# An encoder layer in float32: the residual comes back in eight halves, and VectorE's order is changed where passes meet

## What is computed

```
h = rmsnorm(x, mix_norm_g)
x = x + forgetting_attention(h, ...)          # called x1 below
h = rmsnorm(x, ffn_norm_g)
gate, up = split(h @ w_gu)                    # 2048 -> 2 * 5632
x = x + (silu(gate) * up) @ w_down            # 5632 -> 2048
```

## Time and profile before

| what | value |
|---|---|
| median of 3 runs | 2190.46 us (2188.57 to 2190.71) |
| the profiled execution's own time | 2189.52 us |
| its span in the profile | 2187.8 us |
| TensorE busy | 2129.5 us, 97% of the span |
| TensorE weight loads busy | 1852.7 us, 85% |
| VectorE busy | 1524.6 us, 70% |
| ScalarE busy | 915.4 us, 42% |
| GpSimd busy | 183.8 us, 8% |
| granted TensorE clock, mean | 0.992 |

### The profile page before, as it was taken

One profiled execution on the slowest core, in us unless ns is written; L12 is line 12 of the kernel. 1 busy time (PEld: TensorE's weight loads), 2 busy tenths in 40 slices (PEclk: granted clock), 3 DMA queues, 4 the chain that ended last, 5 costly groups with the idle time before them and its releaser, 6 DMA issues.

```text
span 2187.8 us, 27845 instructions
## 1 busy us (share of the span) xinstructions
PE 2129.5 (97%) x10404; PEld 1852.7 (85%) x10404; DVE 1524.6 (70%) x2103; ACT 915.4 (42%) x1225; POOL 183.8 (8%) x356
## 2 busy tenths in 40 slices
PE   9999999999999999999999999999999989999997
PEld 8999999999998887888888888888887777777786
DVE  4544444444464445987888888788798888898888
ACT  5433333333343334444444444444445534444432
POOL 0322213222230000000000000000000001000000
PEclk9999999999999999999999999999999999999999
DMA  6332333333343335566566566567668757757755
GB/s 181 88 92 82 88 85 90 85 89 81 92 144 135 116 106 163 178 226 220 179 222 226 177 219 229 190 207 228 193 207 280 261 201 270 236 177 250 234 175 178
DMA packets 258331, 376.30 MB, mean 172 GB/s; under 512 B 15762, under 2 KB 114100, under 8 KB 257220
## 3 DMA queue, kind: packets, MB, share of 16 engines
q1 hardware_dynamic: 254864, 354.90, 51.6%
q10 hardware_dynamic: 3380, 20.21, 2.2%
HBM read 346.45 MB, written 28.61 MB: 171 GB/s over the span
## 4 chain that ended last, share of the span: by engine, by line
PE 83%; DVE 9%; DMA 6%; issue 1%; SPq 1%; POOL 0%; ACT 0%; DVEq 0%; POOLq 0%; ACTq 0%
PE gemm L522 11%; PE gemm L524 11%; PE gemm L523 11%; PE gemm L723 8%; PE gemm L725 8%; PE gemm L724 8%; PE aux L723 7%; PE aux L725 7%; PE aux L724 6%; DVE f_lo L1344 4%; DMA f_raw<-in_ffn_w_gate_up 3%; DMA f_raw<-in_ffn_w_down 2%; DVE f_raw L1350 2%; PE aux L523 1%; PE aux L524 1%; PE aux L522 1%
## 5 line engine op out<-in xcount | busy, mean ns | idle before, releaser
L1344 DVE TENSOR_TENSOR f_lo<-f_raw,f_hi 128x2048 fp32r<-128x2048 f32 (+1 forms) x264 | 534.2, 2030 | 63.9 <-ACT f_hi L1007 51.4
L522 PE MATMUL gemm<-w_hi,act_t 128*128 128x384 f32 (+2 forms) x1280 | 450.6, 352 | 1.6 <-DVE w_lo L1123 1.6
L524 PE MATMUL gemm<-w_hi,act_t 128*128 128x384 f32 (+2 forms) x1280 | 444.0, 347 | 0.0
L523 PE MATMUL gemm<-w_lo,act_t 128*128 128x384 f32 (+2 forms) x1280 | 443.9, 347 | 0.0
L723 PE MATMUL gemm<-f_hi,a_form 128*128 128x512 f32 x1056 | 412.4, 391 | 0.4 <-DVE rows L1428 0.4
L724 PE MATMUL gemm<-f_lo,a_form 128*128 128x512 f32 x1056 | 411.7, 390 | 0.0
L725 PE MATMUL gemm<-f_hi,a_form 128*128 128x512 f32 x1056 | 411.3, 389 | 0.0
L723 PE MATMUL aux<-f_hi,a_form 128*128 128x512 f32 x792 | 318.3, 402 | 42.8 <-DVE f_lo L1344 42.8
L725 PE MATMUL aux<-f_hi,a_form 128*128 128x512 f32 x792 | 312.2, 394 | 0.0
L724 PE MATMUL aux<-f_lo,a_form 128*128 128x512 f32 x792 | 311.9, 394 | 0.0
L1123 DVE TENSOR_TENSOR w_lo<-w_raw,w_hi 128x768 fp32r<-128x768 f32 (+1 forms) x160 | 160.8, 1009 | 208.5 <-ACT w_hi L818 208.5
(11 more groups left out here) (161 smaller groups left out, 2143.0 us busy)
## 6 DMA issues: line engine op xcount, KB each, us to landing
f_raw<-in_ffn_w_gate_up SPq DMA_DIRECT2D x264, 512.0 KB, 4.2
f_raw<-in_ffn_w_down SPq DMA_DIRECT2D x132, 512.0 KB, 4.8
w_raw<-in_fox_w_in SPq DMA_DIRECT2D x192, 256.0 KB, 3.4
f_raw<-in_ffn_w_gate_up SPq DMA_DIRECT2D x88, 256.0 KB, 4.0
w_raw<-in_fox_w_out SPq DMA_DIRECT2D x16, 1024.0 KB, 5.1
a_raw<-forms_scratch SPq DMA_DIRECT2D x22, 512.0 KB, 6.3
f_raw<-in_ffn_w_down SPq DMA_DIRECT2D x44, 256.0 KB, 4.8
forms_scratch<-fa_a ACTq DMA_DIRECT2D x11, 896.0 KB, 6.3
```

Of the source, the lines that this page charges most:

```text
L522: mm(out, a_hi, b_hi, start=first, stop=False)
L523: mm(out, a_hi, b_lo, start=False, stop=False)
L524: return mm(out, a_lo, b_hi, start=False, stop=last)
L1344: v.tensor_tensor(f_lo[:, n % 4, 0:3 + g], f_raw[:, n % 4, 0:3 + g], f32(f_hi[:, n % 3, 0:3 + g]), ALU.subtract).then_inc(f_lo_done, 1)
```

## The change

It has three parts. The staging buffers in `rows` are laid out anew, with a new one, `fa_first`, for the seventh step of round 0. The residual comes back in eight loads of 512 KB, each half a column group, put behind the weight loads of eight different units, from unit 168 (round 10) to unit 195 (round 12). In VectorE's order the turn of the first pass's last unit becomes a meeting turn, and `add_p1` is cut in two: its first addition is made in turn 2 of the second pass, the other (`turn_x4`) stays in turn 4.

```
-        fa_a = at("fa_a", AREA_S, [P, 8, HW])
-        c_one = at("c_one", AREA_S, [P, 2, CW])
-        u_two = at("u_two", AREA_S + 4096, [P, 2, CW])
-        fa_b = at("fa_b", AREA_S + 8192, [P, 8, HW])
-        c_neg = at("c_neg", AREA_S + 24576, [P, 2, CW])
+        c_neg = at("c_neg", AREA_S, [P, 2, CW])
+        fa_first = at("fa_first", AREA_S, [P, 8, HW])
+        fa_a = at("fa_a", AREA_S + 8192, [P, 8, HW])
+        c_one = at("c_one", AREA_S + 8192, [P, 2, CW])
+        u_two = at("u_two", AREA_S + 12288, [P, 2, CW])
+        fa_b = at("fa_b", AREA_S + 24576, [P, 8, HW])
...
+            def reload_x1(d, half):
+                ts = slice(2 * half, 2 * half + 2)
+                sp.dma_start(rows[:, d, ts], dram_x1[d][:, ts]).then_inc(x1_ld[d], 16)
...
-                if n == BASE[R_DOWN] + 8:
+                if n == BASE[R_DOWN] - 8:
                     for d in range(ND):
                         sp.wait_ge(x1_stored[d], 16)
+                    reload_x1(0, 1)
+                if n == BASE[R_DOWN] + 6:
+                    sp.wait_ge(hidden_done, 4 * NP)
+                    reload_x1(0, 0)
+                if n == BASE[R_DOWN] + 8:
                     sp.wait_ge(hidden_tr, 4 * NP)
-                    sp.dma_start(rows[:, 2], dram_x1[2]).then_inc(x1_ld[2], 16)
+                    reload_x1(2, 1)
                 if n == BASE[R_DOWN] + 9:
+                    reload_x1(2, 0)
+                if n == BASE[R_DOWN] + 13:
                     sp.wait_ge(forms_stored[0], 16 * NP)
-                    sp.dma_start(rows[:, 0], dram_x1[0]).then_inc(x1_ld[0], 16)
-                if n == BASE[R_DOWN] + 18:
+                    reload_x1(1, 0)
+                if n == BASE[R_DOWN] + 15:
+                    reload_x1(1, 1)
+                if n == BASE[R_DOWN] + 17:
                     sp.wait_ge(forms_stored[1], 16 * NP)
-                    sp.dma_start(rows[:, 1], dram_x1[1]).then_inc(x1_ld[1], 16)
-                    sp.dma_start(rows[:, 3], dram_x1[3]).then_inc(x1_ld[3], 16)
+                    reload_x1(3, 1)
+                if n == BASE[R_DOWN] + 19:
+                    reload_x1(3, 0)
...
-                pool.wait_ge(x1_ld[n], 16)
-                pool.wait_ge(x1_ld[2 + n], 16)
+                pool.wait_ge(x1_ld[n], 32)
+                pool.wait_ge(x1_ld[2 + n], 32)
...
-                x1, x4 = rows[:, n, 0:2], rows[:, 2 + n, 2:4]
+                x1 = rows[:, n, 0:2]
                 v.tensor_tensor(x1, x1, junk_act[:], ALU.add).then_inc(x1_p12, 1)
+
+            def turn_x4(r):
+                n = (r - R_DOWN) % 2
+                x4 = rows[:, 2 + n, 2:4]
                 v.tensor_tensor(x4, junk_act[:], x4, ALU.subtract).then_inc(x4_p1, 1)
...
-                meeting = (g == 0 and j == ROUND_K[r] - 2) or (g == 1 and j == 0)
+
+                form = LOAD_AT.get(n - 4)
+                if g == 0 and j == ROUND_K[r] - 2:
+                    form = None
+                if g == 0 and last and n - 5 in LOAD_AT:
+                    down_forms_lo(*LOAD_AT[n - 5])
+                meeting = (g == 0 and j >= ROUND_K[r] - 2) or (g == 1 and j == 0)
...
+                    if r >= R_DOWN and j == 2:
+                        add_p1(r)
                     if r >= R_DOWN and j == 4:
-                        add_p1(r)
+                        turn_x4(r)
...
-                if n - 4 in LOAD_AT:
-                    down_forms_lo(*LOAD_AT[n - 4])
+                if form:
+                    down_forms_lo(*form)
```

More of the change, by code:

```diff
@@ L950, in form_read @@
                 if q >= 6:
-                    act.wait_ge(x1_stored[q - 6], 16)
+                    act.wait_ge(x1_stored[7 - q], 16)
                 k = NK + 4 * d + i
@@ L1018, in read_p1 @@
                 if r == 0:
-                    act.wait_ge(x1_stored[0], 16)
+                    act.wait_ge(x1_stored[1], 16)
                     act.wait_ge(aform_lo, 7)
@@ L1053, in hidden_forms @@
                     act.wait_ge(forms_stored[1], 16 * (r - 1))
+                if i == 1 and r == 1:
+                    act.wait_ge(x1_stored[3], 16)
                 for half, pair in ((0, slice(0, 8, 7)), (1, slice(1, 7, 5))):
@@ L1091, in _ @@
                         form_hi(6, fa_a)
-                        form_read(7, fa_b)
+                        form_read(7, fa_first)
                     if r == 0 and j == 3:
-                        form_hi(7, fa_b)
+                        form_hi(7, fa_first)
                     if j == 3 and hidden:
@@ L1367, in second_pass_read @@
                     dve.wait_ge(x1_stored[2], 16)
-                    dve.wait_ge(x1_stored[3], 16)
                 for t in range(2):
@@ L1419, in add_p2_p3 @@
                 if r < R_DOWN + 2:
-                    dve.wait_ge(x1_ld[n], 16)
+                    dve.wait_ge(x1_ld[n], 32)
                 for t in range(2):
@@ L1520, in _ @@
                             form_lo(6, fa_a)
-                            form_sums(7, fa_b)
+                            form_sums(7, fa_first)
                         if j == 3:
-                            form_lo(7, fa_b)
+                            form_lo(7, fa_first)
                             row_sums(1)
```

## The result

| | before | after |
|---|---|---|
| median | 2190.59 us (2188.57 to 2191.37, 4 runs) | 2205.93 us (2201.93 to 2207.18, 4 runs) |
| profiled execution, its span | 2189.52, 2187.8 us | 2205.96, 2204.2 us |
| granted TensorE clock, mean | 0.992 | 0.994 |

The ratio is 1.0068, 95% interval 1.0051 to 1.0086: the change makes the kernel slower, by more than the 0.2% that can be told from nothing. Four executions among those of the experiments, two of them of the kernel before, took 3442 to 5674 us; medians and ratios here leave them out.

What follows compares the result with a forecast made beforehand. TensorE was taken as the bound, busy 2129.5 of 2187.8 us, losing time only through waits, clock or added work. The terms 19.6 - 4.5 - 5.5 = +9.6 us on the 2190.46 us median gave 2200 us, range 2193 to 2209.

Steps and rivals of the forecast that it cites:

- The swap: Where the two passes meet, rounds 0 to 10: `f_lo` goes ahead of the next unit's sums; +19.6 us, ends +15 and +24.
- 2.5 - 1.08: Round 1's meeting: 2.5 us of delay less 1.08 us gained by `f_lo` of the second pass's first unit starting sooner.
- P1's wait: Middle of the second pass's first unit: TensorE waits 1.3 us for ScalarE's late copy of P1.
- The echoes: After P1's wait: TensorE's waits for `f_lo` of the next two units, 0.55 and 0.45 us.
- Round 11, -4.5 us: Round 11: earlier `f_lo` and load, and part of the slow clock won back; -4.5 us, ends -2 and -7.
- GpSimd's two additions take 2.38 each: Round 11's meeting: after the last half's estimated landing at 1752.5, both additions end at 1757.3.
- on an engine with room inside the pass: 0: VectorE: the first addition of `add_p1` moves two turns ahead, the same 1.22 us each, costing 0.
- Rounds 12 to 16, -5.5 us: Rounds 12 to 16: meeting waits replaced by shorter ones, -2, and slow clock gone, -3.5; ends -2 and -9.
- "Everything else", 0: Moved `add_p1`, spread loads, new places in `rows`, four more loads: counted 0; by the skill's batching advice up to 8 us.
- P1's copy is not late: Rival: P1 is read in time at the meetings, so all the gain stays; 2161 us, chance 0.07.
- Only P1's wait, no echoes: Rival: VectorE and ScalarE absorb the delay inside the second pass's first unit; 2188 us, no change, chance 0.09.
- The clock falls: Rival: three close waits drop TensorE's clock once a round, +1.6 us each; 2218 us, chance 0.08.

Runs made afterwards that it cites:

- e1_swap_only: The kernel before with one line changed, so that `f_lo` goes ahead of the next unit's sums at the pass meeting in all 17 rounds: 2205.95 us, ratio 1.0077.
- e2_no_swap: The changed kernel without the swap; new places, eight loads and the cut of `add_p1` stay: 2190.94 us, ratio 1.001.
- e3_p1_first: The changed kernel with ScalarE's `read_p1` put ahead of the next unit's `f_hi` at the meeting: 2194.21 us, ratio 1.0022.
- e6: e5_reload_later with GpSimd's four additions made to wait for VectorE's sums at the meeting, the subtraction first: 2189.42 us, ratio 0.9988.
- e7: e6 with ScalarE reading P1 ahead of the next unit's `f_hi` in rounds 11 to 16: 2185.58 us, ratio 0.9977.
- e11: e10_p1_together with the GpSimd wait of e6 for the first pair of additions alone: 2185.87 us, ratio 0.9975.
- e10_p1_together: e5_reload_later with both operations of `add_p1` back at turn j = 4: 2183.61 us, ratio 0.9966.
- e8_before_late_swap: The kernel before with the swap in rounds 11 to 16 and nothing else: 2185.66 us, ratio 0.997.
- e9_no_swap_reload_later: The changed kernel without the swap, and the reload of half (0, 1) moved from unit 168 to 172: 2186.59 us, ratio 0.9983.
- e5_reload_later: The changed kernel with the swap in rounds 11 to 16 only and the reload of half (0, 1) moved from unit 168 to 172: 2185.26 us, ratio 0.9973.

## Why the prediction was right, and where not

The forecast was 2200 us, slower, within 2193 to 2209; 2205.93 was measured. The difference foretold was +9.6 us, that of the medians is +15.3, that of the profiled executions +16.4.

- **The swap, +19.6 us: +22.1.** Mechanism and times are those of the prediction: five moments of round 1 agree within 0.05 us. Round 1 grew by 1.46 us where 2.5 - 1.08 = 1.42 was worked out. e1_swap_only and e2_no_swap show that the rest of the change costs nothing beside it. Rounds 1 to 9 grew by 2.0 us each, not by 1.8; both ends of +15 and +24 hold it. The recorded waits of rounds 0 to 10 grow by 12.6 us only, from 11.1 in 12 to 23.7 in 40 (the 22.6 in 39 shown above and the one behind 1700 us). Part of the rest is what every interruption adds beside the idle time on record: round 1's matmul at 957.86 would have started 0.23 after the one at 956.38, so 1.25 us are lost, and 0.34 - 0.23 more until the next; that is 1.36 where the row says 1.10. Twenty-eight more interruptions by 0.26 are 7.3 us; some 2 us stay without a name. The prediction had counted from start to start, so it had this in its sum.
- **How much P1's wait is of it.** It was put at 1.3 a meeting and the echoes at 1.0. The eleven waits are 12.8 us, 1.16 each, and 0.26 that isn't on record, so 1.4. Taking them away gave 1.1 us a round back in e3_p1_first, not 1.4. The echoes stay as they are (0.29 to 0.34 and 0.23 to 0.28 us), but the wait for VectorE's reading of P2 came in, 0.17 to 0.18 on record.
- **Round 11, -4.5 us: -1.7.** This is the term that failed, in two of its steps. `f_lo` of 184 came 2.3 us sooner, measured from the end of round 10 (36.78 against 39.07), predicted 2.6. GpSimd could start 3.9 us sooner, predicted 3.4. From the start of N to that of N + 1, however, 10.7 us were foretold in place of 11.6, and it took 12.4. The first step that failed is "GpSimd's two additions take 2.38 each", and VectorE's sums beside them their usual 0.69: 1.7 us. With that collision taken away (e6, e7, e11) the interval is 10.72, 10.70 and 10.72 us; it is the length foretold, but by another schedule, with GpSimd started later and VectorE waiting for it. The wait of 1.3 for P1 didn't come in round 11, as TensorE ran the six matmuls ahead of it at its lower clock (0.43 us apart in place of 0.23). The second step is "on an engine with room inside the pass: 0". Of the lower clock 1.6 us were counted back, less 0.5 for the echo. The seven slow matmuls of N + 1 did go and N + 1 became 1.2 us shorter, but VectorE has no room in this pass: its turns of 5.81 us took nearly all of it back, and from the start of N + 1 to the end of the round it was 0.2 us less than before (40.43 against 40.66), 0.9 short of the forecast. Where the first operation on P1 stands makes no difference to that sum: with both at j = 4 in e10_p1_together it is 40.47.
- **Rounds 12 to 16, -5.5 us: -4.0.** Within its ends of -2 and -9. The waits at the five meetings, 5.8 us for P1, are there; the one of 2.99 us in round 13 has become 0.97, and of the 22 matmuls that last over 0.56 us in rounds 12 and 13 before none is left (in the whole mixer 23 in after, 52 before). How much of it is the swap's: the kernels with it have 365.9 to 371.5 us in these rounds, the two without 368.6 and 371.3, before 372.1. Swap alone gives it (e1_swap_only 368.0, e8_before_late_swap 365.9), and so does the other change alone (e9_no_swap_reload_later 368.6). Whether the swap adds anything to the halves isn't settled: e5_reload_later has a ratio of 0.9973 with it, e9_no_swap_reload_later 0.9983 without, and their intervals overlap.
- **"Everything else", 0.** P1 in two places: 0, right. The half (0, 1) of x1 at unit 168: 0.5 us at most in the change (round 10 has 82.8 us, in e1_swap_only 82.3), but only since the swap hides it; without the swap it costs 4.4 us in e2_no_swap by the profile, and moved by four units it gives 4.2 and 2.9 us back (e9, e5, each against before on its chip). The prediction let it pass without naming what hides it. The Trainium skill, "DMA: Bandwidth & Descriptors", section "Bandwidth", would have transfers of 1 MiB or more; here no cost of the four loads more shows (e9_no_swap_reload_later, with all eight halves, has 2186.59 us), round 11 became shorter (92.4 us in e2_no_swap against 93.7), and what counted was where in the queue they stood. Size alone, with the same places, was not tested.
- **The rivals.** "P1's copy is not late" falls by the sixteen waits on it. "Only P1's wait, no echoes" falls by e3_p1_first, where the echoes stand alone. "The clock falls" falls by the clock of 0.994 and the slow matmuls: in rounds 0 to 10 there are 10 where before had 9, all in the first unit of round 0.

The miss of 6 us is thus 2.5 from the meetings, 2.8 from round 11, 1.5 from rounds 12 to 16, less some 1 by which the medians lie nearer to each other than the profiled executions.

## What to carry to other kernels

When two pieces of work on one engine change places, follow the one that is now later through every engine that stands behind it, up to the first place where the slowest engine needs it, and then on until the helpers have caught up; here a wait of 1.1 us brought two smaller ones. Order by the meeting at hand: the same swap loses 2.0 us in each of rounds 0 to 9 and loses nothing in rounds 11 to 16, where the loads and not the engines were late. The change with the swap there alone, and one reload moved, is faster than the kernel before (2185.26 against 2191.27 us on the same chip). A transfer put between the loads of two units that are both waited for cost 4.4 us there and nothing that shows four units later. And time won on the slowest engine counts only as far as the next engine has room: in round 11, 1.2 us won in one unit were worth 0.2 at the end of the pass.

## What the runs showed of the hardware

- VectorE's additions with two operands in SBUF and GpSimd's additions in SBUF hold each other up: 0.69 becomes 2.75 us, `a_form` 1.21 becomes 2.20, `f_lo` 2.28 becomes 3.26; GpSimd's 2.38 becomes 2.80. VectorE's additions with an operand in PSUM kept their 1.28 us for two. They take turns. In after, each of VectorE's sums ends 0.55 us after GpSimd's addition beside it (1777.53 and 1776.98, 1780.30 and 1779.74), so it does nearly all its 0.69 behind it. And each of GpSimd's additions, begun while an operation of VectorE from SBUF ran, ends 2.2 us after that one (1776.98 and 1774.73, 1779.74 and 1777.53), nearly its own 2.38 behind it; the first one in e5_reload_later, begun at 1755.73 when VectorE was just through, kept its 2.38. The Trainium skill, "SBUF — State Buffer", section "SBUF: two separate sides", says that VectorE and GpSimd share a pair of ports, and that of an operation of VectorE with two inputs in SBUF and one of GpSimd that reads SBUF the first holds it to its end. The traces agree, and by that rule each of VectorE's sums would have been counted up to one GpSimd addition longer in round 11.
- The DMA that carries the second half of the weights of round 10's N + 1 lands after 4.9 to 5.7 us in seven kernels and after 7.3 or 7.6 in two, with the same requests ahead of it on SyncE's queue. ScalarE's store of `forms_scratch` was issued 3.4 to 4.7 us behind it in all nine, and what sets the one or the other is open. One such landing at a meeting is 3 to 4 us of the whole, in one round or another: e5_reload_later has one in round 4 (82.0 us), e11_all_four in round 9 (83.1). A single profile tells therefore what a step does, but not the time of a kernel within 4 us.
